# Block transpositions for the values of an attention layer, with the way to token order through memory

## What is computed

```python
h = _rms_norm(x, g_mix)
z = h @ w_in
a, b, q, k, v, qi, ki, wi, ga, gb = jnp.split(z, SPLIT_POINTS, axis=-1)
...
kg = k[sel]
vg = v[sel]
s = jnp.einsum('qhd,qkhd->qhk', q, kg, preferred_element_type=jnp.float32) * (HEAD_DIM ** -0.5)
s = jnp.where(valid[:, None, :], s, -jnp.inf)
p = jax.nn.softmax(s, axis=-1)
o = jnp.einsum('qhk,qkhd->qhd', p.astype(v.dtype), vg)
...
k_p.append(k)
v_p.append(v)
```

## Time and profile before

| | us |
|---|---|
| median of three runs (2063.21 to 2065.27) | 2063.65 |
| profiled execution | 2065.28 |
| its span | 2063.7 |
| TensorE busy in the span | 2044.8 |
| VectorE busy | 1111.3 |
| ScalarE busy | 824.0 |
| one body of W_HEAD | 48.7 |

### The profile page before, as it was taken

How to read it: one execution, slowest core, us unless ns; L and a number is a source line. 1 busy time by engine, 2 the same in 40 slices (tenths; PEclk the granted TensorE clock), 3 DMA queues, 4 the chain that set the end, 5 groups by cost and what they waited for, 6 DMA issues and landing times.

```text
span 2063.7 us, 37734 instructions
## 1 busy us (share of the span) xinstructions
PE 2044.8 (99%) x13945; PEld 2026.5 (98%) x13945; DVE 1111.3 (54%) x1642; ACT 824.0 (40%) x1165; POOL 55.6 (3%) x71
## 2 busy tenths in 40 slices
PE   9999999999999999999999999999999999999997
PEld 8999999999999999999999999999999999999997
DVE  6865777777765443433556444444444333344454
ACT  5633344455446333333344333333333332233343
POOL 2200000000020000000000000000000000000000
PEclk9999999999999999999999999999999999999998
DMA  6445565555645445454445454454454444454443
GB/s 198 122 144 158 150 158 156 146 154 148 160 128 156 143 153 155 150 152 142 133 152 153 154 159 139 149 158 139 150 159 146 142 156 149 143 154 141 142 134 110
DMA packets 337645, 306.20 MB, mean 148 GB/s; under 512 B 51743, under 2 KB 334455, under 8 KB 337600
## 3 DMA queue, kind: packets, MB, share of 16 engines
q1 hardware_dynamic: 335488, 300.07, 48.6%
q0 software_dynamic: 2080, 5.52, 0.8%
q10 hardware_dynamic: 32, 0.01, 0.0%
HBM read 297.36 MB, written 8.19 MB: 148 GB/s over the span
## 4 chain that ended last, share of the span: by engine, by line
PE 97%; DVE 1%; DMA 1%; issue 0%; ACT 0%; SPq 0%; DVEq 0%; ACTq 0%
PE M L583 26%; PE M L585 26%; PE M L584 26%; PE T L584 5%; PE T L585 5%; PE T L583 5%; DMA x_tok<-in_x_prompt 1%; PE T L773 0%; PE S L740 0%; PE S L904 0%; DVE w_lo L1316 0%; DVE c_all L1662 0%; PE S L738 0%; PE S L739 0%; PE S L651 0%
## 5 line engine op out<-in xcount | busy, mean ns | idle before, releaser
L1316 DVE TENSOR_TENSOR w_lo<-w_raw,w_hi 128x1024 fp32r<-128x1024 f32 (+1 forms) x556 | 670.7, 1221 | 560.1 <-ACT w_hi L947 546.5
L947 ACT ACTIVATE w_hi<-w_raw 128x1024 fp32r<-128x1024 f32 (+1 forms) x556 | 573.6, 1051 | 555.0 <-PE M L585 375.6
L583 PE MATMUL M<-h_hi,w_hi 128*128 128x320 f32 x1792 | 561.3, 313 | 2.6 <-DVE w_lo L1316 2.5
L585 PE MATMUL M<-h_hi,w_lo 128*128 128x320 f32 x1792 | 554.3, 309 | 0.0
L584 PE MATMUL M<-h_lo,w_hi 128*128 128x320 f32 x1792 | 554.2, 309 | 0.0
L583 PE MATMUL M<-o_hi,w_hi 128*128 128x320 f32 x1664 | 513.5, 309 | 0.0
L585 PE MATMUL M<-o_hi,w_lo 128*128 128x320 f32 x1664 | 513.1, 308 | 0.0
L584 PE MATMUL M<-o_lo,w_hi 128*128 128x320 f32 x1664 | 513.1, 308 | 0.0
L583 PEld LDWEIGHTS M<-h_hi,w_hi 128*128 128x128 f32 x1792 | 337.1, 188 | 4.9 <-issue 4.4
L584 PEld LDWEIGHTS M<-h_lo,w_hi 128*128 128x128 f32 x1792 | 337.2, 188 | 0.5
L585 PEld LDWEIGHTS M<-h_hi,w_lo 128*128 128x128 f32 x1792 | 336.9, 188 | 0.0
(11 more groups left out here) (311 smaller groups left out, 1302.9 us busy)
## 6 DMA issues: line engine op xcount, KB each, us to landing
w_raw<-in_w_in SPq DMA_DIRECT2D x208, 512.0 KB, 3.9
w_raw<-in_w_gate SPq DMA_DIRECT2D x88, 512.0 KB, 4.4
w_raw<-in_w_up SPq DMA_DIRECT2D x88, 512.0 KB, 4.5
w_raw<-in_w_down SPq DMA_DIRECT2D x88, 512.0 KB, 3.4
w_raw<-in_w_attn_out SPq DMA_DIRECT2D x32, 512.0 KB, 4.8
w_raw<-in_w_out SPq DMA_DIRECT2D x32, 512.0 KB, 3.4
w_raw<-in_w_conv_out SPq DMA_DIRECT2D x16, 512.0 KB, 3.7
x_tok<-in_x_prompt SPq DMA_DIRECT2D x4, 512.0 KB, 9.1
```

The source lines that it names most:

```text
L583: mm(out, w_hi[:, s, wc:wc + m], x_hi, start=start, stop=False)
L585: done = mm(out, w_lo[:, s, wc:wc + m], x_hi, start=False, stop=stop)
L947: act_fn(w_hi[:, s, 0:n], w_raw[:, s, 0:n], ACT.Copy).then_inc(hi_ready, 1)
L1316: v.tensor_tensor(w_lo[:, s, 0:n], w_raw[:, s, 0:n], w_hi[:, s, 0:n].bitcast(f32), ALU.subtract)\
```

## The change

The values go the way of the keys. VectorE transposes each value tile in 32x32 blocks directly out of its accumulator bank, to `v_blocks` (which takes the place of `vT`), in unit 11 of the body: the first tile ahead of that unit's low half, the second behind it. SP stores the blocks (sixteen DMAs of 128-byte runs for a pair, behind loads 6 and 7), waits behind load 8 until they have landed, and loads the pair's values from the output tensors into `v_tok`, by token. The key rows move: row 0 stays behind load 5, rows 1 to 3 go behind loads 9 to 11. The step "values" on TensorE, ScalarE's copies to `vT` and `v_tok`, and POOL's stores are gone; banks M0 and M1 are given back by VectorE (`v_blocks_ready`), and "out" waits for the loads (`v_full`).

```diff
-        HEAD_STEPS = (None, "scores 0", "scores 1", "values", None, "probs 0", "out 0", "probs 1", "out 1")
+        HEAD_STEPS = (None, "scores 0", "scores 1", None, None, "probs 0", "out 0", "probs 1", "out 1")
+        K_OUT_DMAS = 4 * N_BLOCK_ROWS
+        K_ROW_AT, V_ROWS_AT, V_LOAD_AT = {5: 0, 9: 1, 10: 2, 11: 3}, {6: (0, 1), 7: (2, 3)}, 8
...
+            def store_blocks(p, a_row, x, prompt, sample, done):
+
                 for h in range(2):
+                    sp.dma_start(blocked(prompt[0, 0], p, a_row, h), block_rows(x, a_row, h, 0, TP)).then_inc(done, 16)
+                    sp.dma_start(blocked(sample[0, 0], p, a_row, h), block_rows(x, a_row, h, TP, T)).then_inc(done, 16)
...
+            def load_values(p):
+
+                sp.wait_ge(v_out, V_OUT * p + V_OUT)
+                sp.dma_start(v_tok[:, 0:2, :], values(o["v_p"][0, 0].rearrange("(t p) h d -> p t h d", p=P), p))\
+                    .then_inc(v_full, 16)
+                sp.dma_start(v_tok[TS:P, 2, :], values(o["v_s"][0, 0].rearrange("t (o h) d -> t o h d", o=1), p).rearrange("t o c -> t (o c)"))\
+                    .then_inc(v_full, 16)
+
+            def store_pair(p, u):
+                if u in K_ROW_AT:
+                    sp.wait_ge(k_blocks_ready, 2 * p + 2)
+                    store_blocks(p, K_ROW_AT[u], k_blocks, o["k_p"], o["k_s"], k_out)
+                for a_row in V_ROWS_AT.get(u, ()):
+                    sp.wait_ge(v_blocks_ready, 2 * p + 2)
+                    store_blocks(p, a_row, v_blocks, o["v_p"], o["v_s"], v_out)
+                if u == V_LOAD_AT:
+                    load_values(p)
...
-            def store_values(p):
-
-                pool.wait_ge(t_evac, EVACS * p + 3)
-                pool.dma_start(o["v_p"][0, 0].rearrange("(t p) h d -> p t (h d)", p=P)[:, :, ds(p * NU, NU)],
-                               v_tok[:, 0:2, :]).then_inc(v_out, 16)
-                pool.dma_start(o["v_s"][0, 0].rearrange("t h d -> t (h d)")[:, ds(p * NU, NU)],
-                               v_tok[TS:P, 2, :]).then_inc(v_out, 16)
...
-                elif step == "values":
-
-                    pe.wait_ge(t_evac, EVACS * p + 1)
-                    pe.wait_ge(o_lo_done, 2 * p + 1)
-                    for t in range(2):
-                        for h in range(2):
-                            done = tr(T1[:, t * NU + h * P:t * NU + (h + 1) * P], vT[:, h, t * P:(t + 1) * P],
-                                      ident[:])
-                    done.then_inc(v_T_done, 1)
-                    for h in range(2):
-                        done = tr(T0[:, h * P:(h + 1) * P], vT[:, h, T - P:T], ident[:])
-                    done.then_inc(v_T_done, 1)
...
                     pe.wait_ge(cv_full, 16 * p + 16)
+                    pe.wait_ge(v_full, 32 * p + 32)
...
-                        free = (act_evac, lambda b: at(ACT_EV, W_HEAD, i, b - 1))
+                        free = (v_blocks_ready, lambda b: 2 * i + (b - 1))
...
-                if u == 3:
-
-                    act.wait_ge(v_stored, p + 1)
-                    act.wait_ge(v_T_done, 2 * p + 1)
-                    act_fn(v_tok[:, 0:2, :].rearrange("p t c -> p (t c)"), T1[:, 0:2 * NU], ACT.Copy)\
-                        .then_inc(t_evac, 1)
-                    act.wait_ge(v_T_done, 2 * p + 2)
-                    act_fn(v_tok[TS:P, 2, :], T0[TS:P, 0:NU], ACT.Copy).then_inc(t_evac, 1)
...
-                            evac(W_HEAD, i, u, g, vT, ACT.Copy, wait)
...
-                        act.wait_ge(v_stored, PAIRS + 1)
+                        act.wait_ge(k_out, K_OUT * PAIRS)
+                        act.wait_ge(v_full, 32 * PAIRS)
+                        act.wait_ge(pv_done, H + 1)
...
+            def value_blocks(i, b):
+
+                if not isinstance(i, int):
+                    dve.wait_ge(v_out, V_OUT * i)
+                group_tile(W_HEAD, i, 11, 2, b)
+                v.transpose(v_blocks[:, b, :], SET[0][b][:, 0:T]).then_inc(v_blocks_ready, 1)
+
...
                 for u in range(12):
+                    if u == 11:
+                        value_blocks(i, 0)
                     low_half(W_HEAD, i, u + 2)
+                    if u == 11:
+                        value_blocks(i, 1)
                     attend(i - 1, u)
```

More of the change, by code:

```diff
@@ L120, in chunk_causal_conformer_kernel @@
     act_n = dve_n = grp_n = 0
-    for ph, per_act, per_dve, per_grp in ((W_KI, 3, 0, 1), (W_QI, 2, 0, 1), (W_CONV, 2, 2, 2), (W_HEAD, 6, 0, 3),
+    for ph, per_act, per_dve, per_grp in ((W_KI, 3, 0, 1), (W_QI, 2, 0, 1), (W_CONV, 2, 2, 2), (W_HEAD, 4, 0, 3),
                                           (W_MERGE, 4, 4, 4), (W_OUT, 0, 4, 2), (W_UPA, 0, 4, 2), (W_DNA, 0, 2, 1),
@@ L212, in chunk_causal_conformer_kernel @@
         k_sample = sb("k_sample", [P, 2, SK])
-        vT = sb("vT", [P, 2, T])
+        v_blocks = sb("v_blocks", [P, 2, T])
         SW = P + TP + SK
@@ L307, in chunk_causal_conformer_kernel @@
             sem(n) for n in ("conv_tail_T", "conv_rows_ready", "conv_tail_out"))
[L308 to L311, removed]
+        ck_full, cv_full, k_out, v_out, v_full = (
+            sem(n) for n in ("ck_full", "cv_full", "k_out", "v_out", "v_full"))
+        ck_T_ready, scores_done, v_blocks_ready, k_blocks_ready = (
+            sem(n) for n in ("ck_T_ready", "scores_done", "v_blocks_ready", "k_blocks_ready"))
         pT_done, pv_done, t_evac = sem("pT_done"), sem("pv_done"), sem("t_evac")
@@ L360, in load_cached_keys @@
                                     blocked(a["cache_k"][0, 0], p, a_row, h)).then_inc(ck_full, 16)
-        EVACS = 5
+        EVACS = 3
+        V_OUT = K_OUT_DMAS * 16
         CK_FULL = 2 * N_BLOCK_ROWS * 16
-        K_OUT = 4 * N_BLOCK_ROWS * 16
+        K_OUT = K_OUT_DMAS * 16
         @block.sync
@@ L407, in _, with values @@
                     load(W_CONV, i, u, w_in, KU * (u % 4), i * NU + (C_B, C_A)[u // 4], also_next=u == 3, waited=u == 4)
-            def store_keys(p, a_row):
-                sp.wait_ge(k_blocks_ready, 2 * p + 2)
+            def store_blocks(p, a_row, x, prompt, sample, done):
                 for h in range(2):
-                    sp.dma_start(blocked(o["k_p"][0, 0], p, a_row, h), key_blocks(a_row, h, 0, TP)).then_inc(k_out, 16)
-                    sp.dma_start(blocked(o["k_s"][0, 0], p, a_row, h), key_blocks(a_row, h, TP, T)).then_inc(k_out, 16)
+                    sp.dma_start(blocked(prompt[0, 0], p, a_row, h), block_rows(x, a_row, h, 0, TP)).then_inc(done, 16)
+                    sp.dma_start(blocked(sample[0, 0], p, a_row, h), block_rows(x, a_row, h, TP, T)).then_inc(done, 16)
+            def values(x, p):
+                return x[:, :, ds(2 * p, 2)].rearrange("p t h d -> p t (h d)")
+            def load_values(p):
[13 more added lines that the diff above has]
+                    load_values(p)
             def load_head(i, u):
@@ L827, in merge_units @@
                     if g == 0 and isinstance(i, int):
-                        free = (act_evac, lambda b: at(ACT_EV, W_MERGE, 0, b - 1))
+                        free = (v_blocks_ready, lambda b: 2 * PAIRS + (b - 1))
                     if g == 1 and isinstance(i, int) and u == 4:
@@ L1154, in _ @@
                                 .then_inc(conv_rows_ready, 1)
-                    if u % 4 == 3:
+                    if u in (3, 7):
                         g = u // 4
@@ L1159, in _ @@
                         if i0:
-                            wait = ((scores_done, 2 * i), (k_blocks_ready, 2 * i), (v_T_done, 2 * i))[g]
+                            wait = ((scores_done, 2 * i), (k_blocks_ready, 2 * i))[g]
                         if g == 0:
                             evac_queries(i, u, wait)
-                        elif g == 1:
+                        else:
                             evac_keys(i, u, wait)
-                        else:
-                            evac(W_HEAD, i, u, g, vT, ACT.Copy, wait)
                 if i0:
@@ L1630, in _ @@
             for u in range(12):
+                if u == 11:
+                    value_blocks(0, 0)
                 low_half(W_HEAD, 0, u + 2)
+                if u == 11:
+                    value_blocks(0, 1)
                 transpose_blocks(0, u)
```

22 lines of the change are left out of this document (7 added, 15 removed).

## The result

| | before | after |
|---|---|---|
| median of 20 runs each, same chips (us) | 2064.98 | 2060.6 |
| lowest to highest | 2062.78 to 2067.59 | 2058.88 to 2063.15 |
| profiled execution | 2065.28 | 2061.11 |
| its span | 2063.7 | 2059.4 |

The ratio is 0.998 with a 95% interval of 0.9974 to 0.9986: 4 us faster, between 2.9 and 5.4. The change does what the sum said of it, and nearly all of it is TensorE's own time.

What follows compares the result with a forecast made beforehand. TensorE, holding 97% of the last-ending chain, was taken to bound the kernel. 7 x 0.656 + 0 + 0 + 0 = 4.6 us off the median of 2063.65 gave 2059.1 us, range 2057.2 to 2062.2.

Steps and rivals of the forecast that it cites:

- Change 1: Seven loop bodies: six transpositions leave TensorE's back-to-back stream, 0.656 us each body, 4.6 us won in all.
- The eighth step: Same transpositions in the merge: removal gives 0, since TensorE waits there for its low half anyway.
- The clock: Merge, behind the longer wait: 3.40 us at 0.51 clock stays, priced 0; bounds 1.5 us won or lost.
- the fourth rival: Merge: the stretch at the low clock disappears, 6.1 us won, 2057.5 us; chance 0.06.
- Change 2: VectorE's block transpositions free the accumulator banks, 0.5 us each, 0.5 and 0.6 us to spare; price 0.
- such a rival: First rival: 1.0 us block transpositions return banks late, TensorE waits 0.4 us in eight pairs; 2062.2 us, chance 0.10.
- Change 3: SP's queue: values stored and read back in time, 5.6 us to spare in bodies, 1.6 in merge; price 0.
- The second rival: Values come back too late in every pair, stores landing 10 us after issue: 2067 us; chance 0.07.
- Change 4: DMA work: 20,480 more packets of 128 bytes, share from 0.58 to at most 0.71; price 0.
- The third rival: Merge only: stores land in 5.8 us instead of 2.9, values 1.3 us late, 2060.4 us; chance 0.12.

Runs made afterwards that it cites:

- Experiment 1: Changed kernel with the six transpositions put back on TensorE behind unit 3 in all eight places, result unread; median 2064.23 us, ratio to before 0.9998.
- experiment 2: Changed kernel with the six transpositions put back only in the merge's first body, result unread; one execution, 2062.23 us.
- experiment 4: Changed kernel with the wait for the stores and the two value loads moved from behind load 8 to behind load 9; one execution, 2062.23 us.
- experiment 5: Changed kernel with the value loads moved from behind load 8 to behind load 10 and its key row; median 2072.09 us, ratio to before 1.0037.
- Experiment 3: Changed kernel with the first value tile's block transposition moved behind the low half of unit 13, beside the second; median 2066.63 us, ratio to before 1.0006.
- experiment 7: Changed kernel with the two squares of c_all in the merge's first body moved from GpSimd to ScalarE; median 2059.11 us, ratio to before 0.9971.

## Why the prediction was right

**The forecast against the time.** It took 4.6 us off and gave 2059.1 us; 2060.6 was measured. The step was right: the profiled execution was put at 2060.7 and is 2061.11. That the profiled execution came so close is in part luck: +2.04 us in the start-up and -1.53 in the merge, neither foreseen, nearly cancel. Of the 1.5 us between forecast and median, 1.3 are what the step was subtracted from, a median of three runs (2063.65), where twenty runs give 2064.98. A median of three carries such an error with a scatter of single runs over 4 us. The change is 0.21% of the time, on the very line between faster and same, as the chances (0.52 and 0.41) had it.

**Change 1.** 0.656 us per body were worked out, 0.649 measured (341.39 - 336.85, over seven). Experiment 1 gives it back by adding the matmuls alone. This step could be so exact because both sides of it were a steady stream on TensorE.

**The eighth step.** Waits of about 0.7 and 2.7 us were named, 0.75 and 2.52 found (the second is 2.67 by the distance of the starts); experiment 2 shows the start of unit 4 unmoved. The clock was the mis-sized term: the text kept a stretch at 0.5 in the sum because the longer wait kept its place. The wait did, and the stretch did not come. Experiments 2, 4 and 5 have it behind the same wait, 1 and 3 do not. So it was a term of scatter, 1.5 us either way, and the fourth rival, which priced it as an effect of the change, has no support in these traces. The 2.04 us at the start are scatter too, but there the traces show what goes with it. The kernels of the experiments have the same start-up as after. Seven of the ten traces have waits of 0.6 to 1.0 us for `hx_lo` and no low stretch behind it (first scores at 259.2 to 260.3 us). In the other three (the kernel after and experiments 2 and 4) ScalarE waited 1.5 to 2.3 us for the first small weight piece (at most 0.3 us in the seven), TensorE 2.2 to 2.4 us for `hx_lo`, and the low stretch followed (first scores at 261.5 to 261.7). Why that piece landed later was not followed.

**Change 2.** 0.5 us per block transposition out of an accumulator were taken from a nearby row, 0.516 are the median. 0.5 and 0.6 us to spare became 0.46 and 0.69. Experiment 3 shows the deadline to be where the text put it, and prices a miss: 0.81 us per body where the wait reads 0.55 to 0.6. Whoever prices such a rival by the lateness of the release has to add the slower start behind it, some 0.1 us.

**Change 3.** The text gave 5.6 us to spare in the bodies; it is 8.3. The stores land in 2.3 us (2.9 were taken), so that SP's wait for them is all but empty; the value loads take 3.9 and not 3.3. For the merge 1.6 us to spare were given. The trace has 620.00 - (614.34 + 4.0) = 1.7, experiment 4 about 1.5. The extra semaphore of the products with the values shows no time. The second rival's point of decision was 5.6 us of lateness; experiment 5, with its loads behind load 10, sends them out some 9.7 us later (424.52 against 413.96, less 0.9 by which its body starts later), past the 8.3, and loses 0.74 us per body.

**Change 4.** The DMA share went to 0.64, the bound was 0.71. By DMA share, 0.64 x 48.05 x 16 less 0.58 x 48.70 x 16 is 40 us of engine time for 14,487 - 11,525 = 2,962 packets more, 13.5 ns each (about 10 by the share of 0.62 in the bodies of experiments 1 and 3; a share of two digits leaves some 3 ns either way), a third of the average that served as bound. The weight loads of `in_w_in` land in 3.9 us as before. The third rival took 5.8 us for the landing of the stores. With 7,964 packets under 512 bytes in a body instead of 5,232 the value stores land in 2.3 us, sooner than the key stores did. The key stores of 32 KB take 3.2 us at the median where they took 2.9; over all key stores the median stays at 2.9 and the longest has grown from 3.4 to 4.7 us. So the third rival did not happen. The rule of the Trainium skill that transfers under 512 bytes miss line rate ("DMA: Bandwidth & Descriptors", Specifications) gives no size for the landing; the 5.8 us were the prediction's own, and whether such stores run below line rate no run here shows.

## What to carry to other kernels

Work that stands in a steady stream of the engine on the critical path is worth its distance between neighbours' starts (0.656 us worked out, 0.649 measured); the same work ahead of a wait is worth nothing, and there may be a second wait behind the first that covers it too. Moving a layout change from TensorE to block transpositions, with the rest done by the access pattern of a store and a read back, pays if the way back has spare time and the accumulators come free in time: count both against the matmul that asks, and mind on which side of one long operation the release is written. Before a few microseconds are read out of two single traces, cut them into stages and look at the granted clock of each: here 1.5 us came or went with nothing in the change to cause it.

## What the runs showed of the hardware

VectorE and GpSimd hold each other up in the merge, one operation at a time. Started behind an elementwise operation of GpSimd, a low half (128x1024) takes 1.55 to 3.42 us and not 1.22, one subtraction (128x320) 2.60 and not 0.48, an operation on three numbers per partition 1.53 to 2.57 and not 0.17. Their ends fit a hold until GpSimd's operation is over: 610.69 against 610.66 in the kernel after, 607.85 against 607.83 in experiment 7. The low half of 607.26, which started first, kept its 1.21 us, and GpSimd's square took 3.24 us and not 2.3. Not every operation is held: a maximum of 128x256 scores out of an accumulator, at 608.71 within that square, took 0.41 us, as at 600.44 (0.42). Experiment 7 supports the reading for the subtractions, of which none is over 0.49 us since the squares have left GpSimd; what the two share, and which operations need it, was not tried.

A block transposition of 128x320 numbers takes about the same out of an accumulator (504 to 518 ns, median 516) as out of SBUF (468 to 506, median 487), and TensorE writes the bank again right behind it: in experiment 3 the matmul of 399.30 waited for it.

Stretches at the lower clock outside the end of the kernel were 3.4 us long in every execution that had one, in the start-up or in the merge. The one in the merge cost 1.53 us. For the start-up, the same matmuls take 4.56 us in the kernel after (from 15.39 to 19.95) and 2.95 at full clock in experiment 5 (from 14.64 to 17.59): 1.6 us.
